# Outputs split in the attention's last head pair, out2 and the second MLP joined in one program, with entrance and exit by token halves

## The chip, the cores and the metric

The kernel runs on one core of a Trainium2 chip. Its engines work side by side, each from its own list of instructions: TensorE (PE, matmuls), VectorE (DVE), ScalarE (ACT), GpSimd (POOL), and SyncE (SP), which here only issues transfers. They wait for each other by semaphores. The metric is the time of one execution in microseconds (us). Before the change it is 3237.32 us, the median of 3 runs (3236.09 to 3241.56).

## The reference, cut to what matters

The whole reference is two transformer blocks over 1024 tokens and a model width of 1024, in float32. The change lies in the end of the second:

```
def hybrid_mixer(...):
    ...
    o_mla = causal_block_attention(q_mla, k_mla, v_mla, MLA_SCALE)
    o_fox = causal_block_attention(fq, fk, fv, FOX_SCALE, f_cum)
    y = sigmoid(g_mla) * (o_mla @ w_o_mla) + sigmoid(g_fox) * (o_fox @ w_o_fox)
    return y @ w_out

def conv_ffn(h, w_up, conv_w, conv_b, w_down):
    u = h @ w_up                                  # 1024 -> 2 x 2816
    u = conv_b + sum(conv_w[j] * up[:, j:j + s] for j in range(3))   # up: u padded by 2 tokens
    gate, val = u[..., :D_FF_2], u[..., D_FF_2:]
    return (silu(gate) * val) @ w_down

    x = x + g_m * mix                             # mix = hybrid_mixer(...)
    h = modulate(rmsnorm(x, norm_ffn_g), sh_f, sc_f)
    x = x + g_f * conv_ffn(h, ...)
    return rmsnorm(x, norm_final_g)
```

## The kernel before, in words

Activations lie with channels on the 128 partitions and the 1024 tokens along the row; a tensor of 1024 channels is 8 such tiles. A tile is used in two halves of 512 tokens. A product is made of three matmuls: x and the weights are each split into a high part (rounded) and a low part (the rest), and high x high, low x high and high x low are summed. A tile's split is one op on ACT (`..._hi`) and one on DVE (`..._lo`, a subtraction).

Weights come in blocks of 128 x 1024 values (512 KB), 221 in all, in a fixed order. SP loads a block into one of two `w_raw` slots, POOL makes `w_hi` (L274) and `w_lo` (L277) of it, PE uses it for 48 matmuls of 512 tokens (`use_block`, L299). POOL may split block b + 2 only when PE is done with block b, since there are two slots. PE's results stand in 8 banks, 4 pairs of 2 (one pair holds a tile of 1024 tokens); a pair is free once DVE or ACT has read it (`pair_free`).

The stages that the change touches, each a program of its own (`nc.Block()`), at whose end all engines meet:

- MLA attention, four pairs of heads, two units of 512 tokens a pair. PE makes scores, ACT the exps (L2076), DVE sums them (L2133), PE multiplies with v and sums over the tokens (L2042), DVE makes the outputs (L2139).
- o2, 8 blocks of 4 k-tiles and 2 output tiles each (w_o_mla and w_o_fox by turns). First ACT and DVE split all eight output tiles (L2565, L2587) and PE waits for the eighth low part. Then four turns of two blocks: DVE multiplies by the gates (L2596), adds the two (L2601), ACT and DVE split the sum (y2). Gates come from a scratch tensor by SP's queue (turns 0 and 1) and ACT's (2 and 3).
- out2, 8 blocks of 8 k-tiles, one output tile each: residual += ada x product (L2649), squares on ACT, their sum on DVE (L2642).
- second MLP (mlp2), 66 blocks. PE sums the squares over the partitions, DVE and ACT make 1/rms, DVE scales each tile and makes `y_lo` (L488), and PE's first two blocks follow tile by tile (`first_two`, L325). Then eleven chunks: 4 up blocks, convolution, silu, split; and, one chunk behind, 2 down blocks of 8 output tiles, which DVE adds to an accumulator (L2792). The accumulator is set to zero by 8 memsets (L2761) at the start.
- final: DVE merges the accumulator into the residual (L2815, 8 ops), ACT squares (L1314), PE sums (L462), norm, 8 products (L2821), 8 transfers.

Other places in the program already go by halves of the tokens: mlp1 and gate to in2. There the last two blocks (`last_two`, L352) make the first half of both output tiles and then the second, and the next two (`next_two`) start on the first half while the second is still being normed.

## Time and profile before

| what | value |
|---|---|
| profiled execution | 3241.66 us, span 3238.6 us, granted clock 0.959 |
| runs | 3241.56, 3237.32, 3236.09 us |
| PE busy | 3006.3 us (93%) |
| DVE | 1576.3 us (49%) |
| POOL | 1054.9 us (33%) |
| ACT | 791.6 us (24%) |

The span goes from the first to the last instruction, the execution's time has what lies around it too. Busy time is the time in instructions, for PE also at a lowered clock. The page cuts the span into 40 slices of 81 us; PEclk is the clock that PE was granted there, in tenths. A row of a timeline gives the start from the span's beginning, the duration, the engine, the line, output and inputs, and, in brackets, how long the engine had stood idle before and whose work it then waited for. "PEq" as the releaser is PE's own sequencer. Rows with xN put N instructions together.

### The profile page before, as it was taken

What the parts mean: (1) busy time and instruction counts of PE and PEld (TensorE: products, weight loads), DVE (VectorE), ACT (ScalarE), POOL (GpSimd) and SP (SyncE); (2) the same over time, 40 slices, a digit from 0 to 9 for tenths busy, and PEclk for the clock granted to TensorE, in tenths of its full rate; (3) what the DMA queues carried; (4) which work ended last, traced back from release to release, by engine and by line L of the source; (5) the groups of instructions that cost most, each with busy time, mean ns of one, the idle gap of its engine ahead of it and who ended that gap; (6) DMA issues with size and microseconds to landing.
All of it is one profiled execution on the core that took longest, in us unless ns stands there. A gap on an engine that the chain in (4) does not pass through costs nothing. (4 is left out here: it accounts for less than half of the span.)

```text
span 3238.6 us, 34502 instructions
## 1 busy us (share of the span) xinstructions
PE 3006.3 (93%) x13322; PEld 2382.7 (74%) x13322; DVE 1576.3 (49%) x1550; ACT 791.6 (24%) x1044; POOL 1054.9 (33%) x476
## 2 busy tenths in 40 slices
PE   6999997999999998899997996798988999999997
PEld 5876575788888886778886664675776888888885
DVE  3639946445555557731301467455426433343335
ACT  2148833211211223210012243134002111111111
POOL 2330033444444442433434112200333343343431
PEclk9999999999999999999999797699999999999998
DMA  2121031123222222221132411110321111111111
GB/s 103 53 65 27 14 137 40 59 85 103 91 94 100 93 82 85 66 82 48 65 110 92 98 40 46 46 27 1 143 97 33 53 46 52 45 47 50 45 52 58
DMA packets 67430, 216.33 MB, mean 67 GB/s; under 512 B 8848, under 2 KB 15248, under 8 KB 66448
## 3 DMA queue, kind: packets, MB, share of 16 engines
q1 hardware_dynamic: 62368, 196.28, 19.2%
q10 hardware_dynamic: 4976, 18.88, 1.5%
q8 instruction: 57, 0.93, 0.1%
q14 instruction: 29, 0.24, 0.0%
HBM read 170.50 MB, written 22.54 MB: 60 GB/s over the span
## 5 line engine op out<-in xcount | busy, mean ns | idle before, releaser
L274 POOL TENSOR_TENSOR w_hi<-w_raw,inv_count 128x1024 fp32r<-128x1024 f32 x202 | 387.8, 1920 | 1794.7 <-PE ps L299 1176.6
L277 POOL TENSOR_TENSOR w_lo<-w_raw,w_hi 128x1024 fp32r<-128x1024 f32 x202 | 532.8, 2638 | 15.9
L299 PE MATMUL ps<-x_hi,w_hi 128*128 128x512 f32 x1216 | 378.2, 392 | 16.1 <-POOL w_lo L277 10.0
L299 PE MATMUL ps<-x_hi,w_lo 128*128 128x512 f32 x1216 | 376.6, 391 | 0.0
L299 PE MATMUL ps<-x_lo,w_hi 128*128 128x512 f32 x1216 | 376.5, 391 | 0.0
L299 PEld LDWEIGHTS ps<-x_hi,w_hi 128*128 128x128 f32 x1216 | 229.9, 189 | 65.9 <-issue 11.9
L299 PEld LDWEIGHTS ps<-x_lo,w_hi 128*128 128x128 f32 x1216 | 230.0, 189 | 48.1
L299 PEld LDWEIGHTS ps<-x_hi,w_lo 128*128 128x128 f32 x1216 | 229.7, 189 | 48.0
L299 PE MATMUL ps<-y_hi,w_hi 128*128 128x512 f32 x800 | 247.5, 391 | 12.2 <-PEq L2550 9.1
L299 PE MATMUL ps<-hidden_hi,w_lo 128*128 128x512 f32 x832 | 256.1, 389 | 0.0
L299 PE MATMUL ps<-hidden_hi,w_hi 128*128 128x512 f32 x832 | 256.1, 389 | 0.0
L299 PE MATMUL ps<-hidden_lo,w_hi 128*128 128x512 f32 x832 | 256.1, 389 | 0.0
L299 PE MATMUL ps<-y_lo,w_hi 128*128 128x512 f32 x800 | 247.2, 390 | 0.0
L299 PE MATMUL ps<-y_hi,w_lo 128*128 128x512 f32 x800 | 246.9, 390 | 0.0
L2769 DVE SCALAR_TENSOR_TENSOR conv_out<-ps,cols,conv_out 128x1023 f32<-128x1023 f32 x44 | 56.5, 1283 | 326.5 <-ACT conv_out L2716 326.5
L299 PEld LDWEIGHTS ps<-y_hi,w_hi 128*128 128x128 f32 x800 | 150.5, 188 | 44.2 <-issue 9.5
L299 PEld LDWEIGHTS ps<-hidden_hi,w_hi 128*128 128x128 f32 x832 | 156.2, 188 | 32.4
L299 PEld LDWEIGHTS ps<-hidden_hi,w_lo 128*128 128x128 f32 x832 | 156.2, 188 | 32.4
L299 PEld LDWEIGHTS ps<-hidden_lo,w_hi 128*128 128x128 f32 x832 | 156.2, 188 | 32.4
L2716 ACT ACTIVATE conv_out<-ps,cols 128x1024 f32<-128x1024 f32 x44 | 53.1, 1207 | 500.9 <-PE ps L299 492.2
L299 PEld LDWEIGHTS ps<-y_lo,w_hi 128*128 128x128 f32 x800 | 150.7, 188 | 31.5
L299 PEld LDWEIGHTS ps<-y_hi,w_lo 128*128 128x128 f32 x800 | 150.7, 188 | 31.4
(381 smaller groups left out, 4887.0 us busy)
## 6 DMA issues: line engine op xcount, KB each, us to landing
w_raw<-wall SPq DMA_DIRECT2D x221, 512.0 KB, 3.5
ada_raw<-wada SPq DMA_DIRECT2D x48, 512.0 KB, 4.2
gates_scratch<-gate_out ACTq DMA_DIRECT2D x16, 512.0 KB, 2.6
residual<-x_t SPq DMA_DIRECT2D x8, 512.0 KB, 8.9
residual<-x_t SPq DMA_DIRECT2D x2, 2048.0 KB, 9.9
emb_scratch<-emb_out ACTq DMA_DIRECT2D x8, 512.0 KB, 2.6
embedding<-emb_scratch SPq DMA_DIRECT2D x2, 2048.0 KB, 12.5
residual_scratch<-residual SPq DMA_DIRECT2D x1, 4096.0 KB, 11.1
```

What stands on the lines that cost most here:

```text
L274: nc.gpsimd.tensor_tensor(w_hi[:, slot, :], w_raw[:, slot, :], one.to_broadcast([P, S]), ALU.mult).then_inc(w_split, 1)
L277: nc.gpsimd.tensor_tensor(w_lo[:, slot, :], w_raw[:, slot, :], w_hi[:, slot, :].bitcast(F32), ALU.subtract).then_inc(w_split, 1)
L299: last = nc.tensor.matmul(ps[:, banks + c, :], lhs, x[:, k0 + k, c * HALF:(c + 1) * HALF], start=(left == nk * 3 - 1), stop=(left == 0))
L2716: nc.scalar.activation(conv_y[:, half, :], pair(2 * t + half), ACT.Identity, scale=at_col(tile0 + (t + conv_col("conv2", half, 0))), bias= ...
L2769: nc.vector.scalar_tensor_tensor(out=y[:, 1:S], in0=z[:, 0:S - 1], scalar=at_col(tile0 + (t + conv_col("conv1", half, 0))), in1=y[:, 1:S], ...
```

## The change

Attention, o2, out2, mlp2 and final become one program, in which each engine runs its stages one after the other without meeting the others (`in_turn`).

- The eight output tiles are split within the last head pair: from step 37 on, one high part behind an exp on ACT (`o_high`), one low part a step later on DVE (`o_low`); the eighth follows the last output. The order of o2's blocks changes to fox first, and its first tiles take bank pairs 1, 2, 0, 3. Gates and the residual (in 8 pieces) all come by SP's queue, between the weights.
- out2's first two blocks take k 0 to 5 of both blocks and then k 6 and 7 of both. Its last two go by halves of the tokens, as do mlp2's first two. The memsets move into out2.
- In mlp2's last chunk the merges (8 ops) stand ahead of the eight adds of the last but one pair of down blocks, and these adds go into the residual at once; the last two down blocks go by halves, with squares, sums, norm and output (16 pieces) by halves.

What stands in DVE's list at the last head pair, before the change (`mla_q` are the MLA outputs, `mla_p_sum` the sums of the exps):

```order
L2133 TENSOR_TENSOR mla_p_sum_10936<-mla_p_sum_10936,mla_p_10934 128x1024 [waits p_added,exp_done]
L2133 TENSOR_TENSOR mla_p_sum_10936<-mla_p_sum_10936,mla_p_10931 128x1024 [waits p_added,exp_done]
L2133 TENSOR_TENSOR mla_p_sum_10936<-mla_p_sum_10936,mla_p_10932 128x2x384 [waits p_added,exp_done]
L2133 TENSOR_TENSOR mla_p_sum_10936<-mla_p_sum_10936,mla_p_10933 128x2x256 [waits p_added,exp_done]
L2133 TENSOR_TENSOR mla_p_sum_10936<-mla_p_sum_10936,mla_p_10934 128x2x128 [waits p_added,exp_done]
L2139 TENSOR_TENSOR mla_q<-ps,mla_inverse 128x512 [waits pv_done,inv_done]
L2450 UNCONDITIONAL_BRANCH
L2581 UNCONDITIONAL_BRANCH [waits barrier_Pool_Activation_PE_DVE_SP_release]
L2587 TENSOR_TENSOR o_mla_lo<-mla_q,o_mla_hi 128x1024 [waits tile_hi] x4
L2587 TENSOR_TENSOR o_fox_lo<-in_raw,o_fox_hi 128x1024 [waits tile_hi] x4
```

and after:

```order
L2140 TENSOR_TENSOR mla_p_sum_10921<-mla_p_10916,mla_p_10917 128x1024 [waits sum_full,exp_done]
L2483 TENSOR_TENSOR o_mla_lo_10936<-mla_q,o_mla_hi_10932 128x1024 [waits o_hi]
L2140 TENSOR_TENSOR mla_p_sum_10921<-mla_p_sum_10921,mla_p_10918 128x1024 [waits p_added,exp_done]
L2483 TENSOR_TENSOR o_mla_lo_10937<-mla_q,o_mla_hi_10933 128x1024 [waits o_hi]
L2146 TENSOR_TENSOR mla_q<-ps,mla_inverse 128x512 [waits pv_done,inv_done]
L2140 TENSOR_TENSOR mla_p_sum_10921<-mla_p_sum_10921,mla_p_10919 128x1024 [waits p_added,exp_done]
L2483 TENSOR_TENSOR o_mla_lo_10938<-mla_q,o_mla_hi_10934 128x1024 [waits o_hi]
L2140 TENSOR_TENSOR mla_p_sum_10921<-mla_p_sum_10921,mla_p_10916 128x1024 [waits p_added,exp_done]
L2140 TENSOR_TENSOR mla_p_sum_10921<-mla_p_sum_10921,mla_p_10917 128x2x384 [waits p_added,exp_done]
L2140 TENSOR_TENSOR mla_p_sum_10921<-mla_p_sum_10921,mla_p_10918 128x2x256 [waits p_added,exp_done]
L2140 TENSOR_TENSOR mla_p_sum_10921<-mla_p_sum_10921,mla_p_10919 128x2x128 [waits p_added,exp_done]
L2146 TENSOR_TENSOR mla_q<-ps,mla_inverse 128x512 [waits pv_done,inv_done]
```

The low parts stood behind the attention and a barrier; now they stand between its sums, and only the eighth comes after them.

What PE has between the attention's last sums and the first matmuls of o2, before the change:

```order
L2042 MATMUL ps<-mla_p_sum_10936,neg_ones 64x512 [waits exp_done,p_added]
L2042 MATMUL ps<-mla_p_sum_10936,neg_ones 64x512
L2450 UNCONDITIONAL_BRANCH
L2574 UNCONDITIONAL_BRANCH [waits barrier_Pool_Activation_PE_DVE_SP_release]
L299 MATMUL ps<-o_mla_hi,w_hi 128x512 [waits pair_free,w_split,tile_lo]
L299 MATMUL ps<-o_mla_hi,w_hi 128x512
L299 MATMUL ps<-o_mla_lo,w_hi 128x512 x2
L299 MATMUL ps<-o_mla_hi,w_lo 128x512 x2
```

and after:

```order
L2049 MATMUL ps<-mla_p_sum_10921,neg_ones 64x512 [waits exp_done,p_added]
L2049 MATMUL ps<-mla_p_sum_10921,neg_ones 64x512
L2635 MATMUL ps<-o_fox_hi_10924,w_hi 128x512 [waits pair_free,o_lo,exp_done,w_split]
L2635 MATMUL ps<-o_fox_hi_10924,w_hi 128x512
L2635 MATMUL ps<-o_fox_lo_10928,w_hi 128x512 x2
L2635 MATMUL ps<-o_fox_hi_10924,w_lo 128x512 x2
L2635 MATMUL ps<-o_fox_hi_10925,w_hi 128x512 [waits o_lo]
```

The barrier is gone, the first block is a fox block, and each k waits for its own low part alone.

DVE at the last chunk of mlp2 and the end, before the change (L2792 adds to the accumulator; the eight before the branch are those of the last two down blocks):

```order
L2792 TENSOR_TENSOR accumulator_13710<-accumulator_13710,ps 128x1024 [waits tile_full] x3
L2792 TENSOR_TENSOR accumulator_13710<-accumulator_13710,ps 128x1024 [waits w_used]
L2792 TENSOR_TENSOR accumulator_13710<-accumulator_13710,ps 128x1024 [waits tile_full] x3
L2792 TENSOR_TENSOR accumulator_13710<-accumulator_13710,ps 128x1024 [waits w_used]
L2668 UNCONDITIONAL_BRANCH
L2812 UNCONDITIONAL_BRANCH [waits barrier_Pool_Activation_PE_DVE_SP_release]
L2815 SCALAR_TENSOR_TENSOR residual_13425<-accumulator_13710,ada,residual_13425 128x1024 x8
L468 TENSOR_SCALAR mean_square<-ps 128x1024 [waits stat_full]
L2821 SCALAR_TENSOR_TENSOR final<-residual_13425,cols,rstd 128x1024 [waits rstd_ready]
L2821 SCALAR_TENSOR_TENSOR final<-residual_13425,cols,rstd 128x1024 x7
```

and after (L2941 and L2944 are the last tile of the last hidden chunk, L3001 the merges, L2955 adds into the residual, L2969 halves of the last two blocks):

```order
L2941 TENSOR_TENSOR conv_out<-conv_out 128x1024 [waits pair_free,act_step]
L2944 TENSOR_TENSOR hidden_lo<-conv_out,hidden_hi 128x1024 [waits tile_hi]
L3001 SCALAR_TENSOR_TENSOR residual_10947<-accumulator_10948,ada,residual_10947 128x1024 [waits pair_free]
L3001 SCALAR_TENSOR_TENSOR residual_10947<-accumulator_10948,ada,residual_10947 128x1024 x7
L2955 SCALAR_TENSOR_TENSOR residual_10947<-ps,ada,residual_10947 128x1024 [waits tile_full,merged]
L2955 SCALAR_TENSOR_TENSOR residual_10947<-ps,ada,residual_10947 128x1024 [waits tile_full] x2
L2955 SCALAR_TENSOR_TENSOR residual_10947<-ps,ada,residual_10947 128x1024 [waits w_used]
L2955 SCALAR_TENSOR_TENSOR residual_10947<-ps,ada,residual_10947 128x1024 [waits tile_full] x3
L2955 SCALAR_TENSOR_TENSOR residual_10947<-ps,ada,residual_10947 128x1024 [waits w_used]
L2969 SCALAR_TENSOR_TENSOR residual_10947<-ps,ada,residual_10947 128x512 [waits tile_full,pair_free]
```

The merges moved from behind the last add to a place ahead of the eight adds of the last but one pair of down blocks, which stood directly behind the hidden tile's low part before.

```diff
+    if W_AT["o2"] <= b < W_AT["out2"]:
+        return W_AT["o2"] + ((b - W_AT["o2"]) ^ 1)
...
-        for low, high in ((0, W_AT["mlp1"]), (W_AT["mlp1"], W_AT["gate"]), (W_AT["gate"], W_TOTAL)):
+        for low, high in ((0, W_AT["mlp1"]), (W_AT["mlp1"], W_AT["gate"]), (W_AT["gate"], W_AT["o2"]),
+                          (W_AT["o2"], W_AT["out2"]), (W_AT["out2"], W_TOTAL)):
...
+    def o_ready(s):
+
+        n = s - 37
+        return [n] if 0 <= n < 7 else []
+
+    def o_high(act, n):
+        if n < 4:
+            act.wait_ge(*score_full.at(36))
+        else:
+            act.wait_ge(*o_free.at(2 * (n - 4) + 2))
+        nc.scalar.activation(O_HI[n], O_RAW[n], ACT.Identity).then_inc(o_hi.sem, 1)
+
+    def o_low(dve, n):
+        dve.wait_ge(*o_hi.at(n + 1))
+        nc.vector.tensor_tensor(O_LO[n], O_RAW[n], O_HI[n].bitcast(F32), ALU.subtract).then_inc(o_lo.sem, 1)
...
+            for part in q_part(s):
+                high(*part)
+            for n in o_ready(s):
+                o_high(act, n)
...
+            for n in o_ready(s - 1):
+                o_low(dve, n)
...
-            pe.wait_ge(*tile_lo.at(8))
-            for i in range(4):
-                for q, (a, b) in enumerate(((om_hi, om_lo), (of_hi, of_lo))):
-                    use_block(pe, G + 2 * i + q, (G + q) % 2, 4, 2, a, b, 0, 4 * i + 2 * q, 2 * q, 4)
...
+    O2_PAIRS = (1, 2, 0, 3)
...
+    def o2_sync(sp):
+        sp.wait_ge(*pv_done.at(0))
+        load_gates(sp, 0)
+        load_blocks(sp, G2 + 3, G2 + 4)
+        sp.wait_ge(*o_free.at(0))
+        load_gates(sp, 1)
+        for i in (2, 3):
+            load_blocks(sp, G2 + 2 * i, G2 + 2 * i + 2)
+            sp.wait_ge(*pair_free.at(4 * (i - 1)))
+            load_gates(sp, i)
+        load_blocks(sp, GY, GY + 2)
+        sp.wait_ge(*pair_free.at(12))
+        for k in (0, 1):
+            load_residual(sp, k)
+        load_blocks(sp, GY + 2, GY + 3)
+        for k in range(4, 8):
+            load_residual(sp, k)
+        sp.wait_ge(*pair_free.at(16))
+        for k in (2, 3):
+            load_residual(sp, k)
...
+        with before(MLA):
+            o_high(act, 7)
...
+    def o2_tensor(pe):
+        for i in range(4):
+            for q in range(2):
+                b = G2 + 2 * i + q
+                pe.wait_ge(w_split, b * 2 + 2)
+                for m in range(2):
+                    n = 4 * i + 2 * q + m
+                    if n < 3:
+                        with before(MLA):
+                            pe.wait_ge(*consumed(JOBS[last_job(o2_pair(n))]))
+                    elif n == 3:
+                        pe.wait_ge(*o_free.at(0))
+                    pe.wait_ge(*pair_free.at(n - 3))
+                    for k in range(4):
+                        if n in (0, 2):
+                            pe.wait_ge(*o_lo.at(4 * q + k + 1))
+                        for t, (w, xs) in enumerate(((w_hi, O_HI), (w_hi, O_LO), (w_lo, O_HI))):
...
+                    last.then_inc(tile_full.sem if m == 0 else w_used, 1)
...
+    def out2_tensor(pe):
+        def tiles(u, ks):
+            for k in ks:
+                pe.wait_ge(*tile_lo.at(k - 7))
...
+            return last
+        for u in range(2):
+            pe.wait_ge(w_split, (GY + u) * 2 + 2)
+            pe.wait_ge(*pair_free.at(u - 1))
+            tiles(u, range(6))
+        for u in range(2):
+            tiles(u, range(6, 8)).then_inc(w_used, 1)
+        dense(pe, GY + 2, 4, 8, 1, y2_hi, y2_lo, job0=2)
+
+        def stat_0():
+            pe.wait_ge(*square_added.at(8))
+            half_stat(pe, 0).then_inc(stat_full.sem, 1)
+        last_two(pe, GY + 6, y2_hi, y2_lo, 6, stat_0)
...
+            if k in (2, 3):
+                for q in range(4):
+                    nc.vector.memset(acc2[:, 4 * (k - 2) + q, :], 0.0).then_inc(acc_zero.sem, 1)
...
+        next_two(pe, GN, x2_hi, x2_lo, {3: stat_1})
+        use_block(pe, GN + 2, GN % 2, 8, 1, x2_hi, x2_lo, 0, 2, 2, 4)
+        pe.wait_ge(*rstd_ready.at(4))
+        use_block(pe, GN + 3, (GN + 3) % 2, 8, 1, x2_hi, x2_lo, 0, 3, 3, 4)
...
+        pe.wait_ge(*tile_lo.at(16 + 22))
+        for c in range(2):
+            for q in range(8):
+                u, m = divmod(q, 4)
+                b = GN + 64 + u
+                if c == 0 and m == 0:
+                    pe.wait_ge(w_split, b * 2 + 2)
+                if c == 0 and q < 4:
+                    pe.wait_ge(*pair_free.at(121 + q))
+                elif q >= 4:
+                    with after(MLP2):
+                        pe.wait_ge(*residual_ready.at(8 * c + q - 3))
+                for k in range(2):
...
+                last.then_inc(w_used if c == 1 and m == 3 else tile_full.sem, 1)
+                if c == 1 and q == 3:
+                    final_stat(pe, 0)
+        final_stat(pe, 1)
...
+
+    def final_stat(pe, c):
+        with after(MLP2):
+            pe.wait_ge(*residual_ready.at(8 * c + 8))
...
-            down(G + 64, 124, 0, 22)
...
+        def down(i, n, into_residual=False):
...
+                    if into_residual:
+                        nc.vector.scalar_tensor_tensor(out=res2[:, k, :], in0=pair(m), scalar=ada_col(5, k),
+                                                       in1=res2[:, k, :], op0=ALU.mult, op1=ALU.add
+                                                       ).then_inc(pair_free.sem, 1)
+                    else:
+                        nc.vector.tensor_tensor(acc2[:, k, :], acc2[:, k, :], pair(m), ALU.add
...
+        def last(n):
...
+            with after(MLP2):
+                nc.vector.scalar_tensor_tensor(out=res2[:, q, half(c)], in0=ps[:, 2 * (q % 4) + c, :], scalar=ada_col(5, q),
+                                               in1=res2[:, q, half(c)], op0=ALU.mult, op1=ALU.add
+                                               ).then_inc(residual_ready.sem, 1)
...
+            hidden(*chunk_args(4, 0))
+            down(4, 0)
+            hidden(*chunk_args(4, 1))
+            dve.wait_ge(*pair_free.at(116))
+            for k in range(8):
+                nc.vector.scalar_tensor_tensor(out=res2[:, k, :], in0=acc2[:, k, :], scalar=ada_col(5, k),
+                                               in1=res2[:, k, :], op0=ALU.mult, op1=ALU.add).then_inc(merged.sem, 1)
+            dve.wait_ge(*merged.at(8))
+            down(4, 1, True)
+        dve.wait_ge(*pair_free.at(124))
+        for n in range(16):
+            last(n)
+            if n >= 2:
+                total(n - 2)
+        total(14)
...
-            for k in range(8):
-                nc.vector.scalar_tensor_tensor(out=res2[:, k, :], in0=acc2[:, k, :], scalar=ada_col(5, k),
-                                               in1=res2[:, k, :], op0=ALU.mult, op1=ALU.add
-                                               ).then_inc(residual_ready.sem, 1)
...
+        with after(MLP2):
+            for c in range(2):
+                dve.wait_ge(*rstd_ready.at(2 * c + 2))
+                for k in range(8):
+                    write(k, c)
...
+    def final_sync(sp):
+        for c in range(2):
+            for k in range(8):
+                sp.wait_ge(*written.at(8 * c + k + 1))
+                sp.dma_start(out[:, k, half(c)], final[:, k, half(c)]).then_inc(stored.sem, 16)
+        sp.wait_ge(*stored.at(256))
...
+            in_turn(pe, (mla_tensor, MLA), (o2_tensor, O2), (out2_tensor, OUT2), (mlp2_tensor, MLP2))
```

## Rows read from the trace of the kernel before

**Rows 1.** Timeline, end of attention to o2: start us, us, engine, line, operation, [idle <- releaser]

```profile
2257.78 1.03 PE L2042 MATMUL ps<-mla_p_sum,neg_ones 128*64 128x512 f32 x4
...
2262.23 7.69 DVE L2587 TENSOR_TENSOR o_mla_lo<-mla_q,o_mla_hi 128x1024 fp32r<-128x1024 f32 x4 [1.39 <-ACT o_mla_hi L2565]
...
2269.84 4.62 DVE L2587 TENSOR_TENSOR o_fox_lo<-in_raw,o_fox_hi 128x1024 fp32r<-128x1024 f32 x4
...
2274.52 1.22 PE L299 MATMUL ps<-o_mla_hi,w_hi 128*128 128x512 f32 x2 [15.71 <-DVE o_fox_lo L2587]
```

**Rows 2.** Stretches: length, busy of PE, PEld, DVE, ACT, POOL (x count), PEclk, DMA, GB/s

```profile
2258.80:2279.20 20.40, 4.69 (x14) 3.72 (x13) 12.92 (x9) 8.91 (x10) 5.11 (x2) 0.58 0.40 154
...
2279.20:2363.70 84.50, 84.50 (x373) 69.64 (x372) 36.82 (x27) 6.37 (x6) 32.64 (x14) 1.00 0.32 113
...
2363.70:2377.60 13.90, 4.84 (x12) 3.80 (x12) 6.03 (x5) 2.11 (x2) 4.26 (x2) 0.63 0.31 118
```

**Rows 3.** Waits of PE from 2255 to 2510: sum us, times, longest

```profile
PE ps L299 <- PEq L2550: 9.1, 1, 9.1
...
PE ps L325 <- DVE y_lo L488: 7.5, 1, 7.5
```

**Rows 4.** Timeline, out2's last pair of blocks to the MLP's third

```profile
2440.44 0.62 PE L299 MATMUL ps<-y_hi,w_hi 128*128 128x512 f32 x2
...
2451.57 1.90 POOL L274 TENSOR_TENSOR w_hi<-w_raw,inv_count 128x1024 fp32r<-128x1024 f32 x1 [5.65 <-PE ps L299]
...
2452.72 1.82 DVE L2642 TENSOR_TENSOR mean_square<-mean_square,square 128x1024 f32<-128x1024 f32 x1
...
2505.38 0.74 PE L299 MATMUL ps<-y_hi,w_hi 128*128 128x512 f32 x2 [3.10 <-POOL w_lo L277]
```

**Rows 5.** Timeline of ACT and DVE, last head pair

```profile
2250.54 1.02 ACT L2076 ACTIVATE mla_p<-ps 128x1024 f32<-128x1024 f32 x1 [2.67 <-PE ps L1992]
...
2251.60 2.29 DVE L2133 TENSOR_TENSOR mla_p_sum<-mla_p_sum,mla_p 128x1024 f32<-128x1024 f32 x2 [2.47 <-ACT mla_p L2076]
```

**Rows 6.** Costliest groups: POOL's low parts of weights

```profile
L277 POOL TENSOR_TENSOR w_lo<-w_raw,w_hi 128x1024 fp32r<-128x1024 f32 x202 | 532.8, 2638 | 15.9
```

**Rows 7.** Timeline of mlp1's exit and of gate to in2

```profile
1241.16 0.69 ACT L396 ACTIVATE rstd<-ps,cols 128x512 f32<-128x512 f32 x1 [1.22 <-PE ps L392]
...
1340.69 0.39 PE L352 MATMUL ps<-x_hi,w_hi 128*128 128x512 f32 x1
...
1366.17 3.41 DVE L1808 SCALAR_TENSOR_TENSOR x_modulated<-residual,modulation,rstd 128x512 f32<-128x512 f32 x2 [1.97 <-ACT rstd L399]
...
1370.61 0.77 PE L352 MATMUL ps<-x_hi,w_hi 128*128 128x512 f32 x1 [6.85 <-DVE x_lo L1814]
...
1375.07 0.80 PE L352 MATMUL ps<-x_hi,w_hi 128*128 128x512 f32 x1 [2.85 <-DVE x_lo L1814]
...
1377.74 0.80 PE L352 MATMUL ps<-x_hi,w_hi 128*128 128x512 f32 x1 [1.02 <-DVE x_lo L1814]
...
1405.30 1.22 PE L299 MATMUL ps<-x_hi,w_hi 128*128 128x512 f32 x2 [2.49 <-POOL w_lo L277]
```

**Rows 8.** Timeline, last down blocks and final norm

```profile
3166.33 4.61 DVE L2792 TENSOR_TENSOR accumulator<-accumulator,ps 128x1024 f32<-128x1024 f32 x4
...
3169.48 1.89 POOL L274 TENSOR_TENSOR w_hi<-w_raw,inv_count 128x1024 fp32r<-128x1024 f32 x1 [6.51 <-PE ps L299]
...
3180.11 0.62 PE L299 MATMUL ps<-hidden_hi,w_hi 128*128 128x512 f32 x2
...
3203.62 9.66 DVE L2815 SCALAR_TENSOR_TENSOR residual<-accumulator,ada,residual 128x1024 f32<-128x1024 f32 x8 [0.33 <-PEq L2668]
...
3225.22 9.66 DVE L2821 SCALAR_TENSOR_TENSOR final<-residual,cols,rstd 128x1024 f32<-128x1024 f32 x8 [2.21 <-ACT rstd L476]
```

**Rows 9.** DMA issues: operation x count, KB each, median us to landing

```profile
gate_in<-gates_scratch SPq DMA_DIRECT2D x4, 1024.0 KB, 8.8
...
out_t<-final SPq DMA_DIRECT2D x8, 512.0 KB, 3.0
```

More of the change, by code:

```diff
@@ L1935, in _program, with last_job @@
     JOB_NO = {job: n for n, job in enumerate(JOBS)}
+    def last_job(r):
+        return max(n for n in range(len(JOBS)) if n % 3 == r)
     def job_bank(kind, n):
@@ new lines, in res2_add @@
+    def res2_add(dve, k, c=None):
+        if c is None:
+            dve.wait_ge(x_landed[k], 32)
+            wait_tile(dve, GY + k, 1, 0, 0)
+        elif c == 0:
+            dve.wait_ge(x_landed[k], 32)
+            dve.wait_ge(*half_full.at(k - 6 + 1))
+        else:
+            wait_tile(dve, GY + k, 1, 0, 0)
+        cs = slice(0, S) if c is None else half(c)
+        src = pair(k % 2)[:, cs]
+        nc.vector.scalar_tensor_tensor(out=res2[:, k, cs], in0=src, scalar=ada_col(2, k), in1=res2[:, k, cs],
+                                       op0=ALU.mult, op1=ALU.add).then_inc(pair_free.sem, 1)
```

688 lines of the change are left out of this document (373 added, 315 removed).

## Prediction

> **What bounds the kernel now.** I read the busy table first: PE is busy in 93% of the span, no other engine in more than half of it. PE is the bound wherever it has something to do, and a change can only win where PE stands still or runs at half its clock. Then the 40 slices of the page: from the last head pair on, PE falls to 8 tenths in slices 28, 30 and 31 (2186 to 2267 and 2348 to 2510 us) and to 7 in the last; these are the edges of stages that the change touches. All else from 2186 on is 9. (The slices with a granted clock of 6 and 7 tenths lie ahead of them, where nothing changes.) Then the stretches, the waits of PE and the timelines at those edges.
>
> - End of attention to o2: after the last sums (2257.78 and 1.03 us) PE starts o2 at 2274.52, released by the eighth low part [rows 1]. The four o_mla_lo took 7.69 us, the four o_fox_lo 4.62 [rows 1]. Then o2's matmuls go at half clock for a while: from 2274.52 to 2363.70, with 84.50 us for 373 matmuls at full clock, that is 0.2266 us each [rows 2]; o2 has 384, so 87.0, and it took 89.2: 2.1 us for the clock.
> - o2 to out2: PE stands 9.1 us at the edge of two programs [rows 3], and in the 13.90 us from 2363.70 it has 12 matmuls in 4.84 us at a granted 0.63 [rows 2], where 2.7 would do: 2.1 us again. Together 11.2.
> - out2 to MLP: out2's last two blocks begin at 2440.44, the third block of the MLP at 2505.38, after 3.10 us of waiting for its weights' split [rows 4]. Four blocks of 48 matmuls lie between (10.88 us each, 43.5), so 21.4 of the 64.9 us are lost; 7.5 of them are the wait for y_lo, the first normed tile [rows 3].
> - End: the last two down blocks begin at 3180.11 [rows 8]; the end is at 3238.6, 58.5 us later, of which their matmuls are 21.8. The rest is 9.66 us of merges, squares, the norm and 9.66 us of the final products, one after the other [rows 8].
>
> **The change part by part.**
>
> *A, outputs split in the last head pair.* Seven high parts go to ACT behind the exps, seven low parts to DVE. The 15.71 us wait goes, with the clock loss that it causes. PE goes from the sums to o2's first tile without a barrier, since that tile now needs only fox parts and a free bank. Saved: 15.7 and 2.1, 17.8. What it adds: 7 ACT ops of about 1.0 us, as the exp there (1.02) and 7 DVE ops of 1.16 (4.62 / 4). In the last steps ACT stood 2.67 us before the exp of 2250.54, and DVE 2.47 before the sums of 2251.60 [rows 5], so nearly every step has room for one op on each. The steps with room hide them; if every high part delayed an exp, it would be 7.4. The split of a weight block by POOL also moves into the attention, 1.90 and 2.64 us [rows 4, 6], in which DVE's adds wait. I take 0.7 for it (between 0 and 1.4). What is late next is the eighth pair of parts: needed only by the last k of o2's second block, a block (10.9 us) later. A: 17.1 saved.
>
> *Queue.* All gates, residual pieces and weights now go through SP's queue in one order. A gate load of 1024 KB lands in 8.8 us [rows 9], and it is issued half a turn (two blocks of o2, 21.8 us) or more ahead. I take nothing; the case where it costs is a rival.
>
> *B, first two blocks of out2.* k 0 to 5 of both go first, so the wait for the last low parts of o2's result (k 6 and 7) is covered by 16.3 us of matmuls. The 11.2 us go. But the first block's weights are now in use until 19.0 us after the start (72 + 12 matmuls), and only then may POOL split the third block: 1.90 + 2.64 [rows 4, 6] end it at 23.6 or so, while PE is done at 21.76. That is a new wait of 1.9; the row nearest to it is the 3.10 us of [rows 4], where both blocks end 0.7 us apart. B: 9.3 saved, 8.1 if the wait is 3.1.
>
> *C, second MLP entered and left by halves.* There is a precedent in the trace, with the same helpers: gate to in2. Its last two blocks begin at 1340.69, its third next block at 1405.30 [rows 7]: 64.6 us, against 64.9 of now. A pure copy would gain 0.3. Its waits of PE are 6.85, 2.85, 1.02 and 2.49 us [rows 7]. The 2.85 and 1.02 come while ACT does a sigmoid and loads its table twice between the first normed tiles; here the squares need no other table, so these two should go: 64.6 - 3.9 = 60.7. The 6.85 I keep: x_modulated took 3.41 us for two halves [rows 7], beside POOL's split, and POOL splits again at just this point. With the clock staying up it would be 58, with more sums between the tiles 64.6. C: 4.2 saved (0 to 7).
>
> *D, the end.* Now 8 merges (residual += gate x accumulator) stand in DVE's order between the last hidden tile and the eight adds of the last but one pair of down blocks, then the adds go into the residual, and the last pair goes by halves with its squares beside it. Before, DVE was free for the adds at 3166.33 [rows 8]. After: 8 merges of 1.21 us (9.66 / 8), 9.7, and beside them POOL's two split ops from 3169.48, 1.89 + 2.4 [rows 8], which DVE has to let pass: 4.2 more. They end at 3180.3 and the first add at 3181.6. The second block's first tile needs the bank of the first block's first tile, so PE stops when it has four tiles, at 3169.3, until 3181.7: 12.4 us, and 2.1 for the clock as at both edges above. The last pair begins 14.5 us late, at 3194.6. Behind the merges nothing else waits on DVE; ACT and SP are idle there.
> From there: PE 21.76 and a sum 0.9, DVE's last add and sums to 25.4 (half operations: about 0.66 us, an estimate from 1.21 / 2 and the fixed part), 8 half products of the first half to 30.6, of the second to 35.9 (its Ln and Exp, 0.69 us each [rows 7], are hidden behind the first), and the last transfer 3.6 (3.0 to land [rows 9], and its issue). 39.5 instead of 58.5 us: 19.0 saved less 14.5, D: 4.5.
>
> **Which of DVE's ops wait for POOL.** The row first: a DVE add of two SBUF tensors took 1.82 us at 2452.72, beside POOL's split from 2451.57 [rows 4], where 1.21 is the merges' mean [rows 8]; o_mla_lo 1.92 on average and o_fox_lo 1.16 [rows 1]. The Trainium skill, "SBUF — State Buffer", section "Who interferes with whom", says that a DVE instruction with two SBUF inputs and a GpSimd instruction that reads SBUF shut each other out for whole instructions, while one with at most one SBUF input is not touched. By that rule the merges and the splits add up in full, as I have them; if the two ran side by side, D would save 4.2 more.
>
> **Sum.** 17.1 + 9.3 + 4.2 + 4.5 = 35.1. The profiled execution took 3241.66 (span 3238.6 and 3.1 around it): 3206.6. The median of the runs is 3237.32, 4.3 below it: 3202.2. I say 3202.
>
> **The rivals.**
> 1. *The merges find room* (14%). If DVE got them done before its bank is wanted, the 14.5 us would not be lost: 3188. For it: nothing but that DVE is busy in 49%. Against: its order is written, and they stand behind the last hidden tile. Half of it, if POOL and DVE ran side by side and the wait were 8.2: 3198; the 14% stand for both.
> 2. *The entrance by halves gains nothing*, as gate to in2: 3206 (15%). For it: 64.6 and 64.9. Against: the two table waits.
> 3. *The splits lengthen the attention*: 7.4 lost of A, 3209 (8%). For it: each step goes from PE over ACT and back to PE, so whatever stands ahead of an exp is felt by PE. Against: the idle 2.67 and 2.47 [rows 5].
> 4. *Slower: a weight block comes late in each turn of o2* (4%). SP's queue is in order, and a weight block's load stands behind waits for gates' slots. Should a gate pair delay the next weights by 10.88 us in each of the four turns, 43.5 is lost, more than all the gains: 3245. It decides once loads of 2 x 8.8 us [rows 9] plus the wait for the slot exceed a turn of 21.8 us. For it: DMA rows of 8.8 us. Against: DMA is busy 0.32 of the stretch [rows 2], and two blocks are ahead.
> 5. *The change doesn't do what it says*: PE still waits for the eighth part at its first block because the order of k doesn't help (3%): 3214.
> My forecast, all as above, has 56%.
>
> **How the numbers follow.** 3202 is the likeliest. Rivals 1, 2 and 3 lie in 3188 to 3209; with the bounds of C (4.2 up, 2.8 down) and B (1.2) 8 in 10 reach from 3190 to 3214: below it the full hiding of the merges, above it rival 4. 0.2% of the time, about what can be told from no change, is 6.5 us: 3230.9 to 3243.8. All cases but the fourth are faster than that: faster 0.95, same 0.01, slower 0.04.
>
> **What would show it.** Right: no wait of PE over 2 us between 2257 and o2's end; o2's clock 1.00 from its start; a wait of PE for w_lo of about 2 us at out2's third block; a wait for y_lo or x_lo of 5 to 7 us with a granted clock near 0.5 to 0.7 behind it at the MLP's entrance; a wait of PE of 12 us, released by the first add into the residual, some 58 us before the end. Wrong: this last wait missing or below 8 us (D mis-sized), exps in the last pair further apart than before (A), a wait of PE for w_lo or of DVE for a gate in o2 (rival 4), over 62 us from out2's last pair to the MLP's third block (C).

## The result

The changed kernel takes 3202.32 us (median of 4 runs, 3201.75 to 3209.44), the kernel before 3236.96 us (median of 4 runs): the ratio estimated from the runs is 0.9897, 95% interval 0.9886 to 0.9909 (the two medians alone give 0.9893). The forecast was 3202. In the three groups of experiments the kernel before had medians of 3237.7 to 3239.1 us (9 to 11 runs each). Two slow executions, one of weights_late with 5353.13 us and one of all_three with 10463.21 us, are left out of the medians and ratios below.

The profiled execution of the changed kernel took 3209.44 us, 7.1 above the median; its span is 3207.7. The head of its page:

```profile
span 3207.7 us, 34389 instructions
PE 2999.0 (93%) x13294; PEld 2380.5 (74%) x13294; DVE 1600.0 (50%) x1598; ACT 796.3 (25%) x1066; POOL 1056.6 (33%) x476
```

PE is busy 7.3 us less than before. Half clock explains that only in part: the mean granted clock is 0.960 against 0.959, and the trace holds 13294 matmuls against 13322. The rest of the 30.9 us of span is time in which PE stood still. What is left of PE's waits is to be seen in its list from 2240 to 3210 us, here without its last row, of 0.7 us (us in all, times, longest):

```profile
PE ps L303 <- DVE residual L2955: 11.7, 1, 11.7
PE ps L356 <- DVE y_lo L2903: 7.1, 3, 5.4
PE ps L303 <- POOL w_lo L281: 4.3, 2, 2.4
PE ps L2892 <- DVE mean_square L2981: 3.1, 1, 3.1
```

The waits of 15.7 and 9.1 us [rows 1, 3] are gone. The wait for y_lo, 7.5 us in one piece before [rows 3], is 7.1 us in three pieces now. The timeline of the edges, in the order of the program:

```profile
2263.25 1.03 PE L2049 MATMUL ps<-mla_p_sum,neg_ones 128*64 128x512 f32 x4
2264.21 0.73 PE L2635 MATMUL ps<-o_fox_hi,w_hi 128*128 128x512 f32 x2
...
2351.38 0.62 PE L2680 MATMUL ps<-y_hi,w_hi 128*128 128x512 f32 x2
...
2375.14 0.93 PE L303 MATMUL ps<-y_hi,w_hi 128*128 128x512 f32 x2 [1.84 <-POOL w_lo L281]
...
2420.40 0.39 PE L356 MATMUL ps<-y_hi,w_hi 128*128 128x512 f32 x1
...
2448.87 0.77 PE L356 MATMUL ps<-y_hi,w_hi 128*128 128x512 f32 x1 [5.42 <-DVE y_lo L2903]
...
2479.03 0.72 PE L303 MATMUL ps<-y_hi,w_hi 128*128 128x512 f32 x2 [2.42 <-POOL w_lo L281]
...
3139.97 13.37 DVE L3001 SCALAR_TENSOR_TENSOR residual<-accumulator,ada,residual 128x1024 f32<-128x1024 f32 x8
3143.11 2.28 POOL L278 TENSOR_TENSOR w_hi<-w_raw,inv_count 128x1024 fp32r<-128x1024 f32 x1 [6.49 <-PE ps L303]
3145.46 3.20 POOL L281 TENSOR_TENSOR w_lo<-w_raw,w_hi 128x1024 fp32r<-128x1024 f32 x1
...
3154.71 1.22 PE L303 MATMUL ps<-hidden_hi,w_hi 128*128 128x512 f32 x2 [11.69 <-DVE residual L2955]
...
3168.44 0.39 PE L2880 MATMUL ps<-hidden_hi,w_hi 128*128 128x512 f32 x1
```

The stretches between them, against those of before, are the balance of the change. (Before, the third block of out2 started at 2396.92, four blocks of 10.88 us ahead of 2440.44 [rows 4]; o2 ended at 2363.70 [rows 2], after at 2351.38.)

| stretch | before | after | saved | forecast |
|---|---|---|---|---|
| A: attention's last sums to the end of o2 | 105.92 | 88.13 | 17.8 | 17.8 (17.1 with POOL's split) |
| B: to out2's third block | 33.22 | 23.76 | 9.5 | 9.3 |
| to out2's last pair | 43.52 | 45.26 | -1.7 | 0 |
| C: to the MLP's third block | 64.94 | 58.63 | 6.3 | 4.2 |
| MLP to the end of the span | 733.2 | 728.7 | 4.5 | 4.5 |
| ahead of the last sums | 2257.78 | 2263.25 | -5.5 | 0 |

The first five add up to 36.4. The sixth is a surprise; 30.9 are left in the profiled executions, 34.6 in the medians. A stretch is measured in one execution of each kernel, and two executions can differ where nothing was changed: at 2125 us, ahead of the first place where the change shows, the changed kernel is 1.26 us behind the kernel before and out2_early 2.33 us ahead of it.

What stands behind most of the sixth: POOL splits the second block of o2's weights at 2144, as soon as its work for the last head pair is done, some 117 us before the point where the barrier held it back. DVE's `mla_neg_max` had to wait for it, and PE for that:

```profile
2144.06 3.21 POOL L278 TENSOR_TENSOR w_hi<-w_raw,inv_count 128x1024 fp32r<-128x1024 f32 x1
2147.35 2.34 POOL L281 TENSOR_TENSOR w_lo<-w_raw,w_hi 128x1024 fp32r<-128x1024 f32 x1
...
2148.55 1.18 DVE L2120 TENSOR_SCALAR mla_neg_max<-stat 128x8 fp32r<-128x8 f32 x1
...
2149.99 0.94 PE L2028 MATMUL ps<-ident,mla_neg_max 128*128 128x128 f32 x4 [1.73 <-DVE mla_neg_max L2122]
```

Before, the same DVE operation took 0.17 us and PE waited 0.73. The Trainium skill, "SBUF — State Buffer", section "Who interferes with whom", names `tensor_scalar` among the operations that can take the port pair shared with GpSimd, and the one who comes second stands still for the whole instruction. The trace agrees: the 128x8 operation ends 0.04 us after POOL's. The prediction gave this section in a shorter form, in which a DVE operation with at most one SBUF input is never touched; this one has one such input and took 1.18 us instead of 0.17. Behind this wait the clock fell to 0.51 for 7 us (2150.00 to 2157.00). The changed kernel's lag behind the kernel before grows there from 1.26 to 5.46 us: 1.0 us is the longer wait and 3.2 the half clock. Of the 7.1 us between the profiled execution and the median these 3.2 are placed; where the rest lies stays open. The 1.26 us were there earlier and have no cause in the change that the traces show.

### The profile page after: what moved, and what is told of

It is laid out like the page before. It is cut to its first block and busy times, and to the rows that moved or that the text cites. A ratio compares the mean times of both kernels' runs of the same rounds, so it can differ in the third digit from the quotient of the medians.

```text
span 3207.7 us, 34389 instructions
## 1 busy us (share of the span) xinstructions
PE 2999.0 (93%) x13294; PEld 2380.5 (74%) x13294; DVE 1600.0 (50%) x1598; ACT 796.3 (25%) x1066; POOL 1056.6 (33%) x476
## 5 line engine op out<-in xcount | busy, mean ns | idle before, releaser
L303 PE MATMUL ps<-hidden_hi,w_hi 128*128 128x512 f32 x800 | 247.6, 391 | 11.7 <-DVE residual L2955 11.7
L303 PE MATMUL ps<-hidden_hi,w_lo 128*128 128x512 f32 x800 | 247.2, 390 | 0.0
L303 PE MATMUL ps<-hidden_lo,w_hi 128*128 128x512 f32 x800 | 247.2, 390 | 0.0
L303 PE MATMUL ps<-y_hi,w_hi 128*128 128x512 f32 x736 | 227.5, 390 | 4.3 <-POOL w_lo L281 4.3
L303 PE MATMUL ps<-y_lo,w_hi 128*128 128x512 f32 x736 | 227.3, 390 | 0.0
L303 PE MATMUL ps<-y_hi,w_lo 128*128 128x512 f32 x736 | 227.0, 390 | 0.0
L303 PEld LDWEIGHTS ps<-hidden_hi,w_hi 128*128 128x128 f32 x800 | 150.8, 189 | 43.4 <-DVE residual L2955 12.1
L1549 DVE TENSOR_TENSOR down_sums<-down_sums,ps 128x1024 f32<-128x1024 f32 x112 | 132.9, 1214 | 73.2 <-PE ps L303 73.2
L303 PEld LDWEIGHTS ps<-y_hi,w_hi 128*128 128x128 f32 x736 | 138.3, 188 | 33.7 <-POOL w_lo L281 2.8
L303 PEld LDWEIGHTS ps<-y_lo,w_hi 128*128 128x128 f32 x736 | 138.7, 188 | 28.9
```

Source lines behind the costliest of these rows:

```text
L303: last = nc.tensor.matmul(ps[:, banks + c, :], lhs, x[:, k0 + k, c * HALF:(c + 1) * HALF], start=(left == nk * 3 - 1), stop=(left == 0))
L1549: nc.vector.tensor_tensor(acc[:, 4 * u + m, :], acc[:, 4 * u + m, :], pair((m + at) % 4), ALU.add).then_inc(pair_free.sem, 1)
```

## The experiments

All against the kernel before, on the same chip within a group. Medians of 3 to 5 runs:

| kernel | us | ratio to before, 95% |
|---|---|---|
| changed, again | 3203.45 | 0.9891 (0.9876 to 0.9906) |
| merges_early | 3186.85 | 0.9845 (0.9832 to 0.9859) |
| out2_early | 3198.19 | 0.9875 (0.9860 to 0.9890) |
| weights_late | 3200.66 | 0.9882 (0.9864 to 0.9900) |
| splits_behind | 3209.67 | 0.9909 (0.9896 to 0.9921) |
| entrance_whole | 3211.13 | 0.9921 (0.9908 to 0.9934) |
| tail_whole | 3188.28 | 0.9852 (0.9840 to 0.9865) |
| all_three | 3184.09 | 0.9832 (0.9819 to 0.9845) |
| barrier_out2 | 3208.82 | 0.9912 (0.9898 to 0.9925) |
| merges_behind | 3199.76 | 0.9881 (0.9866 to 0.9896) |
| four | 3183.60 | 0.9831 (0.9818 to 0.9845) |

The intervals are about 4 us wide to either side (6 for weights_late), so the smaller steps are read from the traces, by the offset: the difference in start between the same instruction of two kernels. Such an offset is that of one execution of each.

**The changed kernel again.**

> The changed kernel again, for a second profile and for the times on this chip. Its profiled execution took 3209.44 us, its other runs 3201.75 to 3202.35. In that profile the granted clock fell to half for some 7 us at 2150 us, behind a wait of PE of 1.73 us where the kernel before had 0.73 and no fall; POOL splits the first block of o2's weights there. Theory 1: the fall is in some executions only, so this profile may lack it, and the median stays at 3202. Theory 2: it is always there, and then the 7 us between the profiled run and the others are spread over other places.

Measured: 3203.45, and its profile (span 3205.8; the other spans 3200.5 to 3202.7) has the fall of the clock once more, 0.51 for 7 us from 2148.20:

```profile
2148.20:2155.20 7.00, 6.96 (x23) 4.24 (x24) 2.81 (x5) 2.07 (x4) 0.00 (x0) 0.51 0.01 1
```

The same stretch of out2_early, which has the same wait of 1.73 us at that point and the same program up to there:

```profile
2146.40:2153.40 7.00, 7.00 (x42) 5.16 (x42) 2.76 (x5) 3.86 (x6) 0.00 (x0) 1.00 0.00 1
```

So the fall comes in some executions only: theory 1, though the second profile didn't lack it. (The expectation calls the block that POOL splits there o2's first; it is the second.) Of the nine profiles of programs that split the block early, each with the wait of 1.73 us, three had the fall (after_same, splits_behind and the changed kernel's first, where this wait ended at 2148.24, 2148.67 and 2149.99) and six had not (it ended at 2145.03 to 2148.49).

**Merges ahead of the last hidden chunk.**

```diff
             down(4, 0)
-            hidden(*chunk_args(4, 1))
-            dve.wait_ge(*pair_free.at(116))
+            dve.wait_ge(*pair_free.at(112))
             for k in range(8):
...
+            hidden(*chunk_args(4, 1))
             dve.wait_ge(*merged.at(8))
             down(4, 1, True)
```

> The eight merges stand ahead of the last hidden chunk on DVE instead of behind it; nothing else differs. My theory: PE's wait of 11.69 us and the 2.85 us at half clock behind it come from the queue position alone, and there is room for 9.7 us of merges and POOL's splits before the first tile of the last up blocks: 3202.3 - 14.5 = 3187.8 us, no wait of PE for the residual over 1 us. Rival: the hidden tiles come late by the 14 us that the merges and splits take together, PE then waits for hidden_lo before its last down blocks, and half or more of the gain is lost: 3195 or above.

Measured: 3186.85, 15 to 17 us less. In its trace DVE's merges take longer, since four of POOL's operations (3080.78 to 3096.96) and not two lie beside them. The next hidden tile's first step comes right behind, and PE waits for nobody:

```profile
3081.99 16.06 DVE L3000 SCALAR_TENSOR_TENSOR residual<-accumulator,ada,residual 128x1024 f32<-128x1024 f32 x8
3097.97 1.27 DVE L2930 SCALAR_TENSOR_TENSOR conv_out<-ps,cols,conv_out 128x1023 f32<-128x1023 f32 x1
```

PE has no wait for the residual any more. Against out2_early, which has the same program from out2's third block to the merges, this execution lags by 3.18 us until the merges and leads by 11.27 us at the first half tile of the last pair, 14.45 us in all. Nothing is added behind that: the spans are 11.3 us apart. The wait and its half clock were a matter of the place in DVE's list alone.

**Merges behind the last whole adds.**

```diff
             hidden(*chunk_args(4, 1))
-            dve.wait_ge(*pair_free.at(116))
+            down(4, 1)
+            dve.wait_ge(*pair_free.at(124))
             for k in range(8):
...
             dve.wait_ge(*merged.at(8))
-            down(4, 1, True)
```

> The eight merges stand behind the adds of the last but one pair of down blocks, which go into the accumulator again; the last pair goes by halves into the residual as before. My theory: what counts is whether a tile of PE's waits behind the merges. Here the fifth half tile of the last pair does, whose bank is free only after the first add behind the merges: merges and POOL's split take 14 us, PE has 5.4 us of work, so it waits 9 to 10.5 us and loses some 2.5 at half clock, about 1.5 to 3 us less than the 14.5 of the changed kernel: 3200 us. Rival: behind the last whole add they are hidden by the last pair's 21.8 us of matmuls, nearly as when early: 3190 us.

Measured: 3199.76. The wait is at the fifth half tile, as said:

```profile
PE ps L2880 <- DVE residual L2969: 9.1, 1, 9.1
```

The merges took 12.34 us there. From the first half tile to the end it is 51.3 us, where merges_early has 39.2: 12.1 us lost, 2.4 less than in the changed kernel. Behind or ahead, work of this length has to stand where no bank of PE's hangs on it.

**out2's first block finished early.**

```diff
-            tiles(u, range(6))
-        for u in range(2):
-            tiles(u, range(6, 8)).then_inc(w_used, 1)
+            tiles(u, range(6) if u == 0 else range(2))
+        tiles(0, range(6, 8)).then_inc(w_used, 1)
+        tiles(1, range(2, 8)).then_inc(w_used, 1)
```

> out2's first block is finished before the second goes beyond k = 1, so its weights are free 13.6 us after the start instead of 19.0. My theory: the wait of PE for w_lo (1.84 us) and the 1.7 us of half clock behind it go, since POOL's split is done at 18.2 and PE at 21.8: 3198.8 us. Rival: the last low parts of o2's result, ready 9.0 us after the start, are needed at 10.9 now, and a new wait takes the old one's place, or the half clock is from something else: 3201 to 3203.

Measured: 3198.19. POOL starts on the third block's weights at 2358.42 and is done at 2362.80, PE goes on without a wait at 2366.34, at full clock (0.61 to 0.62 us for two matmuls):

```profile
2358.42 1.90 POOL L278 TENSOR_TENSOR w_hi<-w_raw,inv_count 128x1024 fp32r<-128x1024 f32 x1 [8.36 <-PE ps L2680]
2360.40 2.40 POOL L281 TENSOR_TENSOR w_lo<-w_raw,w_hi 128x1024 fp32r<-128x1024 f32 x1
...
2366.34 0.61 PE L303 MATMUL ps<-y_hi,w_hi 128*128 128x512 f32 x2
```

Against the changed kernel the timeline has moved by 3.7 us there, 2.0 for the wait and 1.7 for the half clock behind it, and by 0.5 more later. Against merges_early, which has the wait but kept its clock, it has moved by 2.1 and 0.5 us. So some 2.5 us of the gain don't hang on the clock, and 1.7 us come only where it would have fallen.

**o2's second block of weights split behind the attention.**

```diff
     def o2_pool(pool):
+        with before(MLA):
+            pool.wait_ge(*pv_done.at(NA))
         split_weights(pool, G2, 8)
```

> POOL waits for the last products of the attention before it splits the second block of o2's weights; before the change a barrier held it back to that point, now it does it 115 us earlier, beside DVE's maxima. My theory: DVE's neg_max, 1.18 us there instead of 0.17, made PE wait 1.0 us more, and with the half clock that followed it cost 4.9 us in the profiled run. Without it 3201 us if the clock falls only in some executions, 3197.5 if in all. Rival: late, the split (5.1 us) ends too near to the second block, or holds up the last o_mla_lo, and PE waits: 3203 to 3207.

Measured: 3200.66 (3 runs); the wait is 0.72 us again, and the clock doesn't fall:

```profile
2148.57 0.66 PE L2028 MATMUL ps<-ident,mla_neg_max 128*128 128x128 f32 x4 [0.72 <-DVE mla_neg_max L2122]
```

The timeline moves by 1.0 us, and nothing is late in o2. 1.0 us is what the early split costs in every execution; the fall adds 3.2 us in some (the 4.9 us of the expectation should be 4.2). The median fits the first value of my theory, 3201, but its interval is too wide to tell it from no gain.

**Outputs split behind the attention, in one program.**

```diff
-        n = s - 37
-        return [n] if 0 <= n < 7 else []
+        return []
...
-            o_high(act, 7)
+            for n in range(8):
+                o_high(act, n)
...
-        o_low(dve, 7)
+        for n in range(8):
+            o_low(dve, n)
```

> All eight outputs are split behind the attention again, high parts on ACT and low parts on DVE, but still in the one program and still fox first, with PE waiting for one part per k. My theory: the 15.7 us of before came from waiting for all eight behind a barrier; here PE needs only the first part at its start, ready some 4.5 us after the sums, and then goes at the parts' pace of 1.2 us: 4.5 us of waits and 2 of half clock come back, 3202.3 + 6.5 = 3208.8 us. So of A's 17.9 us about 11 belong to the order and the missing barrier, not to the split in the last head pair. Rival: the split in the last pair is what counts, and 15.7 + 2.1 come back: 3220 us.

Measured: 3209.67. PE starts 4.7 us after the sums, not 16.7 [rows 1]:

```profile
2261.92 1.03 PE L2049 MATMUL ps<-mla_p_sum,neg_ones 128*64 128x512 f32 x4
2266.60 0.70 PE L2635 MATMUL ps<-o_fox_hi,w_hi 128*128 128x512 f32 x2 [3.65 <-DVE o_fox_lo L2482]
```

PE's wait is 3.65 us where I had 4.5, and the clock did not fall behind it:

```profile
2266.60:2272.00 5.40, 5.40 (x24) 4.46 (x25) 5.40 (x5) 5.24 (x6) 0.00 (x0) 1.00 1.03 416
```

By the timeline the splits' place is worth 3.7 us at o2; the medians, 6 to 7 us apart with 4 us to either side, don't contradict it. The number came out near 3208.8, but not by the terms that I had: the 2 us of half clock are missing there, and this profile has the fall at 2150 and one more behind the MLP's third block. So of A's 17.8 us some 4 belong to the split in the last head pair, and 14 to the missing barrier, the fox blocks ahead and the wait for one part at a time. These three were not taken apart.

**A barrier again between o2 and out2.**

```diff
-            in_turn(pe, (mla_tensor, MLA), (o2_tensor, O2), (out2_tensor, OUT2), (mlp2_tensor, MLP2))
+            in_turn(pe, (mla_tensor, MLA), (o2_tensor, O2))
...
+    with after(MLA):
+        with after(O2):
+            with nc.Block() as block:
...
+                    in_turn(pe, (out2_tensor, OUT2), (mlp2_tensor, MLP2))
```

(and so on each engine)

> The changed kernel with a second program begun at out2, so that all engines meet between o2 and out2 and out2 can't start before the last low part of o2's result, 9.0 us after o2's last matmul. My theory: B's gain is that the k order covers these 9 us, which only works in one program: 9.1 us and some 2 us of half clock come back at that edge, and the wait for the third block's split stays: 3202.3 to 3203.5 us and 10.5 more, about 3213.5 us. Rival: the gain is from elsewhere (the loads of the residual in pieces), and the barrier costs 1 to 3 us: 3206 us or less.

Measured: 3208.82, 5.4 to 6.5 us more and not 10.5. The stretches at the edge (after the barrier, and behind the wait for the third block), and the wait itself:

```profile
PE ps L2680 <- PEq L3046: 6.5, 1, 6.5
```

```profile
2349.80:2356.00 6.20, 6.16 (x15) 4.89 (x16) 0.00 (x0) 0.00 (x0) 4.27 (x2) 0.53 0.12 23
2376.40:2383.00 6.60, 6.58 (x29) 5.45 (x30) 0.43 (x1) 0.68 (x1) 4.57 (x2) 1.00 0.38 106
```

The expectation was wrong in two places. The barrier costs 6.5 us of wait, not 9.1. DVE's two adds of the last turn and its two low parts follow each other now, where before each low part waited 1.12 us for ACT. And the 9.0 us that I took from the changed kernel have POOL's split of out2's second block beside the two adds, 5.11 us for both; behind the barrier POOL comes later, and they take 2.36. The other place is the clock: behind the barrier it is 0.53 for 6 us, and behind the next wait, of 1.84 us too, it stays at 1.00, where the changed kernel has 0.75 from 2375.10 to 2382.00. That is no work of the barrier, as merges_early keeps 1.00 there without one. Against the changed kernel the offset has grown by 9.5 us up to the third block, and by 7.9 behind the changed kernel's fall. The medians are closer, 5.4 to 6.5 us, with 4 us to either side.

**MLP's entrance by whole tiles.** `last_two` becomes `dense`, `next_two` a loop over k in which both blocks use both halves; scaling, high and low parts go (k, first half), (k, second half).

```diff
-        dense(pe, GY + 2, 4, 8, 1, y2_hi, y2_lo, job0=2)
+        dense(pe, GY + 2, 6, 8, 1, y2_hi, y2_lo, job0=2)
...
-        last_two(pe, GY + 6, y2_hi, y2_lo, 6, stat_0)
...
-        next_two(pe, GN, x2_hi, x2_lo, {3: stat_1})
...
+        for k in range(8):
+            pe.wait_ge(*tile_lo.at(2 * k + 2))
+            for u in range(2):
```

> out2's last two blocks whole and the second MLP's first two blocks tile by tile, with both halves of the tokens of each k ready before it is used; one program as in the changed kernel. From the start of out2's last pair to the MLP's third block it took 58.6 us with halves and 64.9 before. My theory: only part of the 6.3 us belongs to the halves, the rest to the missing barrier and the table load that now lies under other work: 60 to 61.5 us here, that is 3204 to 3205. Rival: it is the halves, and the 6.3 come back: 3208.6 us.

Measured: 3211.13, so the rival, and more. PE's timeline:

```profile
2441.72 3.78 PE L396 MATMUL ps<-mean_square,neg_ones 128*128 128x512 f32 x4 [6.39 <-DVE mean_square L2706]
2450.46 1.19 PE L2849 MATMUL ps<-y_hi,w_hi 128*128 128x512 f32 x2 [4.96 <-DVE y_lo L2899]
...
2477.29 0.74 PE L303 MATMUL ps<-y_hi,w_hi 128*128 128x512 f32 x2 [3.10 <-POOL w_lo L281]
```

PE has no product from 2435.33 (2441.72 less the wait) to 2450.46, 15.1 us, as long as before the change (2462.36 to 2477.51); the sums over the partitions are done at a granted 0.50 and take 3.78 us, and DVE's sums of the last squares lie beside POOL's split (5.03 us for two). The last pair starts at 2413.40: 63.9 us to the third block, 5.3 more than by halves. Behind it the clock falls again (the matmuls at 2479.50 take 1.05 us for two, against 0.62), which makes the whole loss 7.0 us against the changed kernel's timeline. The kernel before has the same wait of 3.10 us there and kept its clock, so this last part need not come back in every execution. The halves gave 5.3 of C's 6.3 us, and all else that changed there, the missing barrier and the table load, 1.0.

**Exit by whole tiles, on top of merges_early.** The loops over q and c change places on PE, DVE and ACT.

> On top of the early merges (3186.9 us): the last two down blocks go tile by tile, both halves of a tile one after the other, so that the first half's norm can't begin before the last tile. Products, squares, norm and output are as many and as large as there. My theory: the halves hide only the first half's Ln, Exp and products behind the second half's matmuls' tail; the writes are held up by DVE in any case until its sums are done, so what comes back is the sum over the partitions, Ln and Exp before the first write, 2.7 us: 3189.6 us. Rival: the exit by halves hides the first half's eight products (5.3 us) too: 3195 us.

Measured: 3188.28 against 3186.85, by the timeline 1.8 us more. DVE's 16 products began 3.0 us after its sums (2.99, for ACT's 1/rms) and, with halves, at once:

```profile
3171.52 10.69 DVE L2984 SCALAR_TENSOR_TENSOR final<-residual,cols,final_rstd 128x512 f32<-128x512 f32 x16 [2.99 <-ACT final_rstd L3036]
```

So of D's 19 us behind the start of the last pair the halves give some 2 (2.7 expected). The rest must come from the merges, squares and norm that no longer stand one after the other behind the matmuls; these were not tested one by one.

**The three edits together, and a fourth.**

> Early merges, out2's first block freed early, and the second o2 block's weights split behind the attention, all in one. The three edits lie in different stretches, so their gains should add: against the changed kernel's 3202.3 to 3203.5 us, 15.5 + 4.3 + 1 less, 3181.5 to 3182.5 us. Rival: an edit that takes a wait away moves the half clock to the next wait, and 3 us or more of it stay: 3185 us or above.

Measured: 3184.09 (5 runs). Against weights_late's timeline the other two edits give 17.4 us from out2's start to the last pair; alone they gave 4.2 and 14.45. Most of the missing 1.3 us is in weights_late: the half clock behind its wait of 11.68 us cost 1.5 us, where it cost 2.6 in out2_early. That the median lies 2 to 3 us above the expected sum is within the intervals. So the gains add within what these runs can tell.

```diff
-        next_two(pe, GN, x2_hi, x2_lo, {3: stat_1})
+        next_two(pe, GN, x2_hi, x2_lo, {1: stat_1})
```

> The three edits together, and the sum over the partitions for the second half of the MLP's entrance one k group after the first step instead of after the fourth. In the trace of the three ACT stands waiting for that sum with the high parts of four tiles behind it in its queue, DVE idles 3.6 us and PE 1.4. My theory: PE's 1.4 us wait goes, PE being the bound behind it: 3184.5 - 1.5 = 3183 us. Rival: the earlier sum stands ahead of matmuls that could run (it needs the last square's add, just done), and PE waits there instead: 3184.5 to 3186 us.

Measured: 3183.60. The wait of 1.4 us is gone, and the second half's 1/rms comes 2.7 us sooner (beyond the 0.35 us by which this whole execution leads all_three's):

```profile
PE ps L356 <- DVE y_lo L2905: 5.6, 2, 5.4
PE ps L2892 <- DVE mean_square L2981: 3.1, 1, 3.1
```

and the MLP's third block starts 2.1 us sooner. But in this profile the clock fell to 0.76 behind the wait of 2.42 us ahead of that block, where all_three kept 1.00, and 0.5 us of the gain are left at the last pair. With the medians 0.5 apart and intervals of 4 us, nothing more is shown. This is the fastest version: 0.9831 of the kernel before (0.9818 to 0.9845).

## Why the prediction was right

- **A** was forecast at 17.8 us without POOL's split, and is 17.8. The splits fit beside the exps: the timelines of the two kernels are 5.46 us apart ahead of the last head pair's splits and 5.47 at the last sums, so the room in the steps did hide them. How much of A is due to them is another matter: splits_behind puts it at 3.7 us.
- **POOL's split** was the one wrong step of A. I put it into the last steps and at 0.7 us. It sits almost 120 us earlier, at the first point where POOL is free, since nothing orders it after the attention. It costs 1.0 us always (weights_late) and 3.2 more when the clock falls.
- **B** was right in the gap (11.2 less a new wait of 1.9; 9.5 measured, the wait is 1.84), and missed that the new wait can have a half clock of its own: 0.75 from 2375.10 to 2382.00, 1.7 us. Net 7.7 in this execution where 9.3 stood. But this term is not always there: of nine profiles with the wait of 1.84 us three have it (the changed kernel twice and weights_late), and six have 1.00. The row that the prediction took as the nearest, 3.10 us, was misread too: the two blocks end one k group of 6 matmuls apart there, some 1.4 us and not 0.7.
- **C** was mis-sized: 60.7 us forecast from gate to in2 [rows 7] less its two waits for tables, 58.63 measured. The waits of 2.85 and 1.02 us did go, the first wait is 5.42 where I kept 6.85, and two others came, 0.21 and 1.47. With the last, 2.42, they add up to 9.5 us, where the forecast kept 9.3 (6.85 and 2.49). So the 2.1 us are not in the waits. They are in the rest, half clock and the sums over the partitions, which is 5.6 us and not the 7.9 of gate to in2. The sign for it came: behind the first wait the granted clock is 0.50 for 5 us.
- **D** was right in each term. The merges end 13.4 us after the hidden tile (13.9), PE's wait is 11.69 (12.4), the half clock behind it 2.85 (13.73 us for 48 matmuls that need 10.88; 2.1 forecast), together 14.5 (14.5); from the last pair to the end 39.3 (39.5). merges_early takes 14.45 of the 14.5 away. The half clock behind this wait was 1.5 to 2.9 us in the seven profiles that have it. The wait ends 53.0 us before the end (3207.7 - 3154.71), not 58 as among the signs; by the prediction's own terms, 3181.7, 3194.6 and 39.5, it is 52.4.
- **Rivals.** The merges didn't find room (1). The entrance did gain (2). Two exps of the last pair came 0.4 to 0.5 us later than the rest, which the next steps made good, so nothing of it is left at the last sums (3). No weight block was late in o2 (4): PE has not one wait there, the only one for a gate is DVE's, 4.16 us ahead of the first multiplication, and PE has other banks. (Two blocks of o2, 21.8 us, are a whole turn, not the half that the paragraph on the queue calls them.) The order of k did its work (5).

C's 2.1 us too little stands against B's 1.6 too much and the 1.0 at 2144, and part of this depends on the execution. The mechanisms were right; that the sum came within 1 us of the median is luck in part.

## What to carry to other kernels

When a barrier is taken away, look at every engine for work that may now start, not only at the one that waited: here POOL moved a split almost 120 us forward, into DVE's way. When a block of vector work is put into a queue, count whose bank is freed by what stands behind it; 14.5 us were lost or not by the place of the same eight operations. And give each new wait of PE a range for the half clock behind it: the same wait of 1.8 us had 1.7 us of it in three profiles and none in six.

## What the runs showed of the hardware that I had not expected

A short wait of PE did not always cost its clock. The wait of 1.84 us ahead of out2's third block was followed by a granted 0.75 in three profiles (the changed kernel twice, weights_late), and by 1.00 in six, among them merges_early, merges_behind, tail_whole and entrance_whole, whose instruction lists are the changed kernel's up to that point. The stretch behind it in the changed kernel and in merges_early:

```profile
2375.10:2382.00 6.90, 6.87 (x23) 5.54 (x24) 0.45 (x1) 0.69 (x1) 4.57 (x2) 0.75 0.39 122
```

```profile
2368.79:2375.69 6.90, 6.90 (x30) 5.72 (x31) 0.42 (x1) 0.67 (x1) 4.56 (x2) 1.00 0.39 109
```

In splits_behind PE kept its full clock after a wait of 3.65 us, and lost it later after one of 2.42; this wait was followed by a fall in two of eleven profiles (the other is four's). The wait of 1.73 us in the attention had the fall in three of nine profiles. As it comes and goes where the program is the same, the program alone does not decide it; what does was not settled. So the half clock behind a wait of 1.8 to 3.7 us stays a range, from 0 to 2 us, and behind the wait of 1.73 us it was 0 or 3.2. And a DVE operation of 8 elements a partition took 1.18 us beside POOL's split, seven times its 0.17.
